# Six changes of order in a two-block transformer kernel, with the overflow path of the experts ahead of their last group

## The reference

```python
mod = silu(c) @ ada_w + ada_b                  # six vectors sh1, sc1, g1, sh2, sc2, g2
h = rms_norm(x, norm_g[0]) * (1 + sc1) + sh1
q, k, v = heads(h @ sb_w_in)
a = where(causal, exp(log_sigmoid(z) + suffix_sum(log_sigmoid(-z))), 0)    # z = q k^T / 8
x = x + g1 * ((a @ v) @ sb_w_out)
h = rms_norm(x, norm_g[1]) * (1 + sc2) + sh2
x = x + g2 * sum_top2(gate * ((silu(h @ w_gate[e]) * (h @ w_up[e])) @ w_down[e]))
x = rms_norm(x, final_g)
x = x + 0.5 * swiglu(rms_norm(x, g_ffn1), w_in1, w_out1)
p = rms_norm(x, g_mix) @ w_mix_in              # q, k, v, o, i, f, z, gate_m, gate_s
h_m = sigmoid(o) * layernorm(mlstm(silu(conv(q, k)), v, i, f)) * head_g
h_s = u * (w_s @ (layernorm(v_s) * norm_g + norm_b) + b_s)                 # u, v_s = gelu(z)
x = x + (sigmoid(gate_m) * h_m + sigmoid(gate_s) * h_s) @ w_mix_out
x = x + 0.5 * swiglu(rms_norm(x, g_ffn2), w_in2, w_out2)
out = rms_norm(x, final_norm_g)
```

## Time and profile before

| | |
|---|---|
| median of 3 runs | 1265.4 us (1263.36 to 1266.26) |
| the profiled execution | 1265.38 us, its span 1263.7 us |
| busy: PE, DVE, ACT, POOL | 84%, 41%, 32%, 3% of the span |
| mean granted PE clock | 0.935 of full speed |
| read from HBM | 356 MB, 283 GB/s over the span |

### The profile page before, as it was taken

One profiled execution on the slowest core, in us unless ns is written; L12 is line 12 of the kernel. 1 busy time (PEld: TensorE's weight loads), 2 busy tenths in 40 slices (PEclk: granted clock), 3 DMA queues, 4 the chain that ended last, 5 costly groups with the idle time before them and its releaser, 6 DMA issues.

```text
span 1263.7 us, 16237 instructions
## 1 busy us (share of the span) xinstructions
PE 1060.8 (84%) x7122; PEld 800.0 (63%) x7122; DVE 514.8 (41%) x610; ACT 402.4 (32%) x483; POOL 39.7 (3%) x69
## 2 busy tenths in 40 slices
PE   6999999555656564738789999999999999999998
PEld 3995594212222121303379999879987778999986
DVE  3544542201102020202074555366844786554543
ACT  2435732000000000000063444354554545544432
POOL 1001200000000000000000000000000220000000
PEclk9999999978778787878999999999999999999999
DMA  9897879999999999999976554456453356455520
GB/s 362 297 382 266 342 301 375 428 428 428 426 428 429 426 427 430 426 426 420 404 242 207 192 201 183 139 203 233 149 185 139 128 200 217 149 185 200 190 111 33
DMA packets 111777, 358.15 MB, mean 283 GB/s; under 512 B 8388, under 2 KB 56152, under 8 KB 97368
## 3 DMA queue, kind: packets, MB, share of 16 engines
q1 hardware_dynamic: 110072, 353.63, 72.3%
q10 hardware_dynamic: 1632, 3.45, 1.0%
HBM read 356.01 MB, written 1.05 MB: 283 GB/s over the span
## 4 chain that ended last, share of the span: by engine, by line
PE 68%; DMA 23%; DVE 5%; ACT 1%; SPq 1%; issue 1%; POOL 0%; DVEq 0%; ACTq 0%
PE psum L2034 17%; PE psum L2036 16%; PE psum L2035 16%; DMA spare<-in_moe_w_down_dram 7%; DMA ring<-in_moe_w_down_dram 5%; DMA spare<-in_moe_w_gate_dram 5%; PE psum L2320 4%; PE psum L2354 3%; DMA spare<-in_moe_w_up_dram 2%; DMA ring<-in_moe_w_up_dram 2%; DMA ring<-in_ada_w_dram 2%; PE psum L2307 2%; PE psum L2267 1%; PE psum L2362 1%; PE psum L2084 1%
## 5 line engine op out<-in xcount | busy, mean ns | idle before, releaser
L1630 DVE TENSOR_TENSOR wl<-ring,wh 128x2048 fp32r<-128x2048 f32 x99 | 227.1, 2302 | 225.6 <-ACT wh L1113 225.6
L1113 ACT ACTIVATE wh<-ring 128x2048 fp32r<-128x2048 f32 x100 | 191.1, 1916 | 301.6 <-PE psum L2036 284.0
L2034 PE MATMUL psum<-hTh,wh 128*128 128x256 f32 x800 | 226.3, 283 | 0.2 <-DVE wl L1630 0.2
L2035 PE MATMUL psum<-hTl,wh 128*128 128x256 f32 x800 | 225.8, 282 | 0.0
L2036 PE MATMUL psum<-hTh,wl 128*128 128x256 f32 x800 | 225.6, 282 | 0.0
L2320 PE MATMUL psum<-ring,m_xT 128*32 128x512 f32 x448 | 98.0, 666 | 66.6 <-DMA spare<-in_moe_w_up_dram 50.7
L2034 PEld LDWEIGHTS psum<-hTh,wh 128*128 128x128 f32 x800 | 152.5, 191 | 0.6 <-DVE wl L1630 0.4
L2036 PEld LDWEIGHTS psum<-hTh,wl 128*128 128x128 f32 x800 | 152.5, 191 | 0.0
L2035 PEld LDWEIGHTS psum<-hTl,wh 128*128 128x128 f32 x800 | 152.5, 191 | 0.0
L2320 PEld LDWEIGHTS psum<-ring,m_xT 128*32 128x32 f32 x448 | 26.0, 121 | 120.4 <-issue 116.7
L1589 DVE TENSOR_TENSOR m_h<-m_sg,psum 128x512 f32<-128x512 f32 x8 | 8.2, 1026 | 214.2 <-PE psum L2320 175.7
(11 more groups left out here) (361 smaller groups left out, 1632.4 us busy)
## 6 DMA issues: line engine op xcount, KB each, us to landing
ring<-in_ffn_w_in_dram SPq DMA_DIRECT2D x44, 1024.0 KB, 7.7
ring<-in_moe_w_down_dram SPq DMA_DIRECT2D x16, 2048.0 KB, 32.9
ring<-in_w_mix_in_dram SPq DMA_DIRECT2D x32, 1024.0 KB, 6.9
ring<-in_moe_w_gate_dram SPq DMA_DIRECT2D x15, 2048.0 KB, 29.2
ring<-in_moe_w_up_dram SPq DMA_DIRECT2D x13, 2048.0 KB, 30.1
ring<-in_ada_w_dram SPq DMA_DIRECT2D x24, 1024.0 KB, 13.1
spare<-in_moe_w_up_dram SPq DMA_DIRECT2D x11, 2048.0 KB, 31.2
ring<-in_ffn_w_out_dram SPq DMA_DIRECT2D x20, 1024.0 KB, 6.6
```

The costliest lines, as they stand in the source:

```text
L1113: a.activation(dst, src, ACT.Copy).then_inc(split_h, 1)
L1630: v.tensor_tensor(split_half(h, wl), raw_half(h), split_half(h, wh).bitcast(FP32), ALU.subtract)\
L2034: t.matmul(dst, sh, mh, start=first, stop=False, skip_group_check=True)
L2035: t.matmul(dst, sh, ml, start=False, stop=False, skip_group_check=True)
```

## The change

1. *Attention, start*: PE waits for the copies of v ahead of stage 2 and not of stage 0.
2. *Attention, pairs 4 to 7*: DVE's subtraction of the two early halves is cut in four pieces (`early_part`), one on each of four stages; before, two whole ones on pairs 4 and 5. The output projection waits for `oTl` feature by feature.
3. *Experts*: the overflow path stands ahead of the last group on all engines, SP's loads included, and uses a copy of `posm`. All wait for `over_done`.
4. *Turn into FFN1*: `x_ready` is given tile by tile, ACT's first split is cut in gate and up, the up part behind the `hTh` copies, and the gate's load has a semaphore of its own. PE's filler products behind the experts are 16 and not 4.
5. *FFN1's end*: ACT copies the first half of `hTh` ahead of the square of tile 1.
6. *Mixer*: scores are made in place in `decay`; those of heads 2 and 3 stand ahead of both splits of their step; the statistics of heads 0 and 1 move to the step before.

```diff
@@ DVE, attention
-                if p in (4, 5):
-                    early_rest(EARLY_QKV + p - 4)
+                if 4 <= p < 8:
+                    early_part(EARLY_QKV + (p - 4) // 2, p % 2)
@@ PE, attention
-            for u in range(2):
-                for tt in range(NT):
-                    await_copied(pe, ("v", u, tt))
             for p in range(PAIRS + 2):
+                if p == 2:
+                    for u in range(2):
+                        for tt in range(NT):
+                            await_copied(pe, ("v", u, tt))
...
-            for p in range(KD):
-                await_copied(pe, ("o", p))
...
-                split_feature_unit([("out", n // 2, n % 2)], next_early, (oTh, oTl))
+                split_feature_unit([("out", n // 2, n % 2)], next_early, (oTh, oTl), parts=None if n else "o")
@@ SP, ahead of the last group's loads (before: behind them)
+            def over_units():
+                sp.wait_ge(r_done, 1)
+                longest = sp.value_load(maxcount, min_val=0, max_val=T)
+                with sp.If(longest > CAP):
+                    sp.wait_ge(main.used, (NEG - 1) * UNITS_PER_GROUP)
...
+                    sp.wait_ge(over_done, 1)
+                sp.end_ifs()
             for n in range(expert_total - 2):
...
+                if n == (NEG - 1) * UNITS_PER_GROUP:
+                    over_units()
@@ DVE, experts
-            for g in range(NEG):
+            for g in range(NEG - 1):
                 if g == 1:
+                    link(v.tensor_copy(posm_over, posm))
...
             dve.end_ifs()
-            dve.sem_inc(x_ready, NT)
+            dve.sem_inc(over_done, 1)
+            expert_steps(NEG - 1, NEG - 1, main, NEG)
+            dve.sem_inc(x_ready, 1)
@@ PE, experts and turn
             pe.end_ifs()
-            keep_busy(psum[:, 7, :], 4)
+            pe.wait_ge(over_done, 1)
+            expert_group(NEG - 1, main, NEG)
+            keep_busy(psum[:, 7, :], 16)
             pe.wait_ge(main.acc, NEG + 1)
             for tt, half in order_of(2):
-                turn(2, tt, half, 3 if (tt, half) == (0, 0) else 1)
+                turn(2, tt, half, 2 if (tt, half) == (0, 0) else 1)
@@ ACT, turn
-                act.wait_ge(x_ready, NT)
                 for tt in range(NT):
+                    act.wait_ge(x_ready, tt + 1)
...
+            def split_first(w):
+                if w == 0:
+                    act.wait_ge(main.used, last_in_ring(RING_B) + 1)
+                    act.wait_ge(first_gate_in, 16)
+                else:
+                    act.wait_ge(wb_in[0], 16)
+                a.activation(split_half(0, wh)[:, :, w, :], raw_half(0)[:, :, w, :], ACT.Copy).then_inc(split_h, 1)
...
-            split_to(1)
+            split_first(0)
             two_norms()
             for tt, half in order_of(2):
                 high_of_hT(2, tt, half)
+            split_first(1)
             b = await_full(act, ("cols",))
@@ ACT, FFN1's end
             root(4, 0)
+            high_of_hT(3, 0, 0)
             square(4, 1, 0)
-            for half in range(2):
-                high_of_hT(3, 0, half)
+            high_of_hT(3, 0, 1)
@@ DVE, mixer
-                if h >= 2:
-                    await_full(dve, ("num", h - 2, 1))
-                emptied(v.scalar_tensor_tensor(sdec[:, h % 2, :], b[:, 0:BLK], MD ** -0.5, decay[:, h, :],
+                emptied(v.scalar_tensor_tensor(decay[:, h, :], b[:, 0:BLK], MD ** -0.5, decay[:, h, :],
...
-            step(mix0 + 10, lambda: score(2), lambda: score(3))
-            step(mix0 + 11, lambda: spatial_norm(0))
+            score(2)
+            score(3)
+            step(mix0 + 10)
+            step(mix0 + 11, lambda: link(head_moments(0)), lambda: spatial_norm(0))
             step(mix0 + 12, lambda: spatial_norm(1), head_stats)
```

More of the change, by code:

```diff
@@ L1733, in _ @@
             down(0, 1, 0)
-            for half in range(2):
-                rest_of_hT(3, 0, half)
+            rest_of_hT(3, 0, 0)
+            rest_of_hT(3, 0, 1)
             down(0, 1, 1)
@@ L2560, in _ @@
                     await_copied(pe, ("s", h))
-                    s = sdec[:, h % 2, :]
+                    s = decay[:, h, :]
                     b = open_bank(pe, ("num", h, 0))
```

90 lines of the change are left out of this document (47 added, 43 removed).

## The result

The changed kernel takes 1256.97 us (median of 6 runs, 1255.24 to 1258.83), the kernel before 1265.83 us beside it (6 runs, 1262.88 to 1269.65). The ratio is 0.9934, 95% interval 0.9916 to 0.9952: 8.4 us less by the ratio, 7.0 us less between the two profiled executions (spans 1256.7 and 1263.7).

A forecast was written before the change was run, and what follows sets the result against it. PE was taken to bound the kernel outside the experts, the DMA weight stream within them; 0.7 + 2.9 + 1.3 + 0 + 0.9 + 1.1 + 0.9 + 1.35 = 9.15 us off 1265.4 gave 1256.2, range 1253.5 to 1261.2.

The forecast's parts named there:

- rivals 3 and 4: Turn gives nothing or loses (-0.8 for 0.9), chance 0.17; clock falls in attention anyway, 1.7 lost, chance 0.12; both 1257.9.
- rival 1: Whole kernel: the forecast itself holds, 1254 to 1259 us; chance 0.56.
- three signs of being wrong: Last down rows under 4 us earlier; new POOL wait at pairs 6 or 7; FFN1 starting on a clock under 1.00.
- (a): Attention's start: PE's wait for copies of v moves to pair 2, ScalarE's table load limits the gain; 0.7 us saved.
- (b): Attention, pairs 4 to 7: halved subtraction shortens PE's mask wait (1.2) and avoids the clock's fall (1.7); 2.9 us saved.
- (c): Output projection's first product: waiting for oTl feature by feature removes the whole wait; 1.3 us saved.
- The stream: Expert weights: the stream waits for slots and moves with PE, so attention's 4.9 us count in full.
- Rival 2: Experts: the weight stream swallows the attention gain of 4.9 us, time 1261.1; chance 0.10.
- The overflow path: Last expert group: PE's jump, up to 5.1 us late, hides behind weight waits; price 0, without cover 5.1 us.
- The turn: Turn into FFN1: the jump's going saves 1.8 us, ScalarE's split half costs 0.96; net 0.9 us saved.
- FFN1's end: FFN1's end: copying the first hTh half ahead of the square removes PE's wait for hTl; 1.1 us saved.
- score: Mixer: head 2's score, made in place and ahead of a split, no longer delays PE; 0.9 us saved.

The follow-up runs named there:

- the second trace of before: The kernel before, unchanged, profiled once more for a second trace; one time of 1262.92 us.
- the late edits alone: The kernel before with only the edits at FFN1's end and in the mixer; 1260.90 us against 1264.39, ratio 0.9976.
- the kernel with attention alone: The kernel before with only the attention edits, parts 1 and 2 of the change; 1261.22 us against 1264.39, ratio 0.9983.
- early rest whole: The changed kernel with the early rest as two whole subtractions on pairs 4 and 5 again; 1257.92 us, ratio 0.9945.
- the run with `cols` first: The changed kernel with ScalarE's copy of cols ahead of the second half of the first split; 1257.69 us against 1264.39, ratio 0.9953.

## Why the prediction was right

The time was forecast as 1256.2 us and measured as 1256.97, inside the range of 1253.5 to 1261.2, and the forecast's mechanisms were there. Its terms hold less well than the sum. The sum itself can't tell them apart, since rivals 3 and 4, both at 1257.9, lie inside the 1254 to 1259 of rival 1; the traces can. Of the three signs of being wrong two didn't come: no new wait on POOL stands at pairs 6 or 7, and FFN1's first product runs at a clock of 1.00. The third, last down rows less than 4 us earlier, depends on the trace: PE's wait for them ends 4.1 us earlier than in the trace that the prediction was made from (628.93 to 624.85), but against the second trace of before A and B together are only 2.4 to 2.7 us shorter. The upper bounds add up to 11.4 us and not 11.8, which moves the range's lower end to 1254.0 and changes nothing else.

- (a) **Attention's start**, 0.7 forecast. From the last v product's end to the adaLN product of stage 1 it was 7.29 us before and is 6.59: 0.70. The wait went to ScalarE's table load and came back at POOL's first mask (0.48 us), as the step from 1.1 to 0.7 said.
- (b) **Pairs 4 to 7**, 2.9 forecast. This is the term that was mis-sized. The wait is 0.70 us (0.6 forecast), the mask 1.39 us long (1.4 forecast), so against a caught mask at full clock the cut gives 1.03 us (49.60 against 48.57), which is its lower bound of 1.2 but for 0.2. The other 1.7 us (1.6 by the two traces of the kernel before), the fall of the clock, was in the one trace that I read and in none of the four others with the whole subtraction. The step that failed is "the clock's fall gone (1.7)": it was priced as certain from one execution. Where POOL's mask of `att_sp` comes first and two of `att_a` are caught in its place, as in the late edits alone, the cut gives 0.3 us (50.92 less 0.70 and 1.34, against 48.57).
- (c) **Output projection**, 1.3 forecast: 1.66 us from the last attention product's start to the first of the projection before, 0.32 after, so 1.34.
- **The stream**, counted in full. Between A and the end of the last down products the lead shrinks by 0.4 us in the changed kernel (473.71 to 474.10). The prediction left nothing for this. Rival 2, that the stream swallows it, is out: the kernel with attention alone keeps 4.3 of 4.7 us against the trace that the prediction was made from, 2.8 of 3.1 against the second one.
- **The overflow path**, priced at 0. Without the move B is 473.7 to 474.1 us in five traces; with it 474.1 to 474.4 in six and, with 18 fillers and the clock fallen behind the up products, 475.1 to 475.3 in three. So it costs about 0.4 us, in some executions 1.3; on the other side stands what it makes possible in the turn. The standstill itself is hidden, as forecast: 3.0 us of it show ahead of the group, and the wait for the last up weights was 6.4 us. The prediction put 5.1 us there and overlooked that PE already stood for 3.1 us in this group (above), where it now stands for 1.4; in all, 4.4 us against 3.1.
- **The turn**, 0.9 forecast. Where the clock fell, it gave nothing to FFN1's first product: 12.09, 12.10 and 12.27 us from the combine in three traces with the new turn, 11.91 to 12.25 in four with the old. In C, with a wait in FFN1's next unit that I hadn't priced, it gave 0.1 to 0.6 us. Where the clock stayed (early rest whole) it gave 0.9 to 1.2 us to FFN1's first product (11.02), which is the forecast, and 1.4 to 1.7 in C, but that trace had lost 1 us in B, where its clock fell instead. The two sides of the sum were right in kind: the second standstill went, and ScalarE's half took its microsecond (0.8 us by the run with `cols` first, 10.24 against 11.02). What was missing is what the prediction named as its risk: PE's idle 2.0 us, and then transposes at 1.2 GHz, 1.1 us of stage C. Rival 3 came true in part: the turn gave less, by the clock.
- **FFN1's end** 1.1, **score** 0.9, **statistics** 1.35 forecast: 1.34, 1.22 and 1.32, in all ten traces to 0.03 us. Where a wait goes wholly, the time falls by it and 0.25 to 0.3 us more: the shown gap runs from the modelled end of a product, and in a chain without a gap the next one begins 0.16 us ahead of this end (0.39 us long, 0.23 us apart, for 512 columns), while the first product behind a wait takes 0.08 to 0.11 us longer to the next one (838.75 to 839.06 before). Of the last wait 0.38 us stays, and it gave just the difference.
- **Not priced**: the clock's fall at the mixer's start, 1.6 us lost in five of ten traces with the late edits, in none of the four without. What decides it the traces don't tell. The late edits alone don't, since five traces with the same mixer don't have it; four traces without them are too few to say that they have no part in it.

By steps that repeat, with the turn taken at the low clock and without the mixer's fall, the change is worth 0.70 + 1.03 + 1.34 - 0.4 + 0.4 + 1.34 + 1.22 + 1.32 = 6.95 us. The measured ratios, 0.9934 and 0.9937 with intervals of 0.0018 to either side, make 8.0 to 8.4, give or take 2.4. The forecast sum of 9.15 is 2.2 too high by those steps: 1.9 in (b), 0.4 in the stream and 0.5 in the turn, less 0.6 for the waits that count more than their gap. The traces themselves give less: from the start of stage A to the end, the two of the changed kernel, both with the mixer's fall, are 4.9 to 7.1 us shorter than the two of before. What makes up the rest of the measured gain I could not see: by (b), executions of the kernel before in which the clock falls in attention add 1.6 us, but how many of the timed ones did is not in the traces. That the median met the forecast within 0.8 us is thus luck for over a microsecond of it: the 6.95 us would have made about 1258.5.

No variant is shown to beat the changed kernel: those with 24 fillers have ratios of 0.9928, 0.9925, 0.9921 and 0.9940.

## What to carry to other kernels

A loss read in one profiled execution is the loss of that execution. Before pricing its removal, ask whether what caused it is fixed by the program (a wait behind an instruction in the same order) or differs between executions of the same code (which of two engines starts first, whether the clock falls behind a wait), and price the second kind by its chance. A table of stage lengths, cut at the same instructions in each trace, tells an edit of 0.3 us, in the stages that repeat, where whole times need 2.

A wait that goes is worth its gap and the restart of the pipeline behind it. A gap moved ahead of a stage with slack is hidden (here all but 0.4 us of it), but look at what was tuned to arrive just in time there, as the filler products of the last group were. And an engine made early hands the wait to the next one in line: the copy of `cols` gained 0.8 us and VectorE's next half took it back.

## What the runs showed of the hardware

- POOL's mask of 0.41 us takes as long as VectorE's subtraction if it begins behind it, 2.46 us behind a whole one and 1.39 behind a half; which begins first differs between traces of the same code: POOL's `att_sp` began 0.27 us behind the whole subtraction in four, 0.18 us ahead of it in one.
- In the mixer the granted clock fell from 2.4 to 1.2 GHz with PE busy for all of the 8 us before (in the changed kernel's trace, 890 to 898 us), 1.1 us behind eight products of 4 rows (1.99 us from 894.80, the fall at 897.9); 1.6 us lost, in five of fourteen traces. That these products bring it on isn't shown: the nine others have them too.
- What comes ahead of attention took 102.5 to 104.1 us in thirteen traces of the same code and 107.2 in one.
- PE's standstill for an untaken branch was 3.57 to 3.62 us behind the experts' last group in five traces; moved ahead of the last group, 3.0 to 3.3 us there in nine traces. Among the last group's products PE also stood without a releaser: 3.1 to 4.1 us in the five, up to 1.4 in the nine.
